# Three places for a split w_q tile, and its low parts summed by a DMA

## What is computed

```python
x = x + g1 * (merged @ w_out[layer])
hffn = rms_norm(x, norm_ffn[layer]) * (1.0 + sc2) + sh2
...
q = (hf @ w_q).reshape(t, PEER_HEADS, 2, PEER_QDIM // 2)     # w_q: 1024 x 2048
s = jnp.einsum('thsd,hskd->thsk', q, subkeys)
top_s, top_i = lax.top_k(s, PEER_TOPK)
...
act = gelu(einsum('thkd,td->thk', u_tab[experts], h)); out = einsum('thk,thkd->td', gate * act, v_tab[experts])
```

## Time and profile before

| | |
|---|---|
| Time, median of 3 runs | 2116.46 us (2115.54 to 2118.68) |
| The profiled execution | 2115.24 us, its span 2113.5 us |
| Granted TensorE clock, mean | 0.989 |
| TensorE busy | 2022.2 us, 96% (weight loads 1734.9 us, 82%) |
| VectorE busy | 1572.1 us, 74% |
| ScalarE busy | 974.8 us, 46% |
| GpSimd busy | 265.2 us, 13% |
| DMA | 392.17 MB, 186 GB/s in the mean |

### The profile page before, as it was taken

How to read it: one execution, slowest core, us unless ns; L and a number is a source line. 1 busy time by engine, 2 the same in 40 slices (tenths; PEclk the granted TensorE clock), 3 DMA queues, 4 the chain that set the end, 5 groups by cost and what they waited for, 6 DMA issues and landing times.

```text
span 2113.5 us, 33847 instructions
## 1 busy us (share of the span) xinstructions
PE 2022.2 (96%) x11108; PEld 1734.9 (82%) x11108; DVE 1572.1 (74%) x3451; ACT 974.8 (46%) x1619; POOL 265.2 (13%) x309
## 2 busy tenths in 40 slices
PE   4998998899999999999999989999999999999998
PEld 3797988788888888888778989898888888888776
DVE  8884888676888888888666358996767676768854
ACT  3223337655444444444532142585555555554443
POOL 2002438400000000000010033590000000000000
PEclk9999999999999999999999999999999999999999
DMA  9376311355778877555443362114555565554562
GB/s 370 143 265 253 119 54 50 106 190 186 271 283 291 307 279 272 205 182 212 168 158 110 120 239 81 66 63 163 188 189 188 207 210 202 185 185 176 178 241 68
DMA packets 115738, 392.17 MB, mean 186 GB/s; under 512 B 12752, under 2 KB 20816, under 8 KB 115152
## 3 DMA queue, kind: packets, MB, share of 16 engines
q1 hardware_dynamic: 115664, 391.21, 51.8%
HBM read 384.35 MB, written 6.82 MB: 185 GB/s over the span
## 4 chain that ended last, share of the span: by engine, by line
PE 67%; DVE 21%; issue 5%; ACT 3%; DVEq 1%; DMA 1%; POOL 1%; SPq 0%
PE ps L890 25%; PE ps L881 13%; PE ps L883 6%; PE ps L624 5%; DVE v_lo L1698 4%; PE ps L852 3%; PE ps L637 3%; DVE next_w_ada_ring L1743 3%; PE ps L766 2%; DVE u_lo L1693 2%; DVE onehot_gate L1677 2%; DVE gated L1706 1%; PE ps L797 1%; ACT gelu L1242 1%; PE ps L792 1%
## 5 line engine op out<-in xcount | busy, mean ns | idle before, releaser
L881 PE MATMUL ps<-h_hi_lo,u_hi 128*128 128x512 f32 x1728 | 630.2, 399 | 6.3 <-DVE u_lo L1693 5.8
L883 PE MATMUL ps<-h_hi_lo,u_lo 128*128 128x256 f32 x1512 | 425.1, 281 | 0.0
L881 PEld LDWEIGHTS ps<-h_hi_lo,u_hi 128*128 128x128 f32 x1728 | 325.9, 189 | 76.6 <-issue 6.5
L883 PEld LDWEIGHTS ps<-h_hi_lo,u_lo 128*128 128x128 f32 x1512 | 286.7, 190 | 8.2
L890 PE MATMUL ps<-v_hi,gated_hi 128*128 128x512 f32 x864 | 271.9, 396 | 5.6 <-DVE gated_lo L1712 4.5
L1693 DVE TENSOR_TENSOR u_lo<-weight_ring,u_hi 128x1024 fp32r<-128x1024 f32 x216 | 263.6, 1221 | 14.9 <-ACT u_hi L1231 11.1
L890 PE MATMUL ps<-v_lo,gated_hi 128*128 128x512 f32 x864 | 268.2, 392 | 0.0
L890 PE MATMUL ps<-v_hi,gated_lo 128*128 128x512 f32 x864 | 266.4, 389 | 0.0
L1698 DVE TENSOR_TENSOR v_lo<-weight_ring,v_hi 128x1024 fp32r<-128x1024 f32 x216 | 263.2, 1218 | 0.6 <-ACT v_hi L1236 0.6
L1236 ACT ACTIVATE v_hi<-weight_ring 128x1024 fp32r<-128x1024 f32 x216 | 227.4, 1053 | 55.6 <-PE ps L890 55.5
L1242 ACT ACTIVATE gelu<-gelu 128x256 f32<-128x256 f32 x216 | 90.3, 418 | 328.3 <-DVE gelu L1702 328.3
(11 more groups left out here) (315 smaller groups left out, 3094.9 us busy)
## 6 DMA issues: line engine op xcount, KB each, us to landing
weight_ring<-in_u_tab_dram SPq DMA_DIRECT2D x224, 512.0 KB, 4.5
weight_ring<-in_v_tab_dram SPq DMA_DIRECT2D x216, 512.0 KB, 3.5
next_w_ada_ring<-in_w_ada_dram SPq DMA_DIRECT2D x56, 512.0 KB, 4.5
weight_ring<-in_w_in_dram SPq DMA_DIRECT2D x46, 512.0 KB, 3.6
w_ada_ring<-in_w_ada_dram SPq DMA_DIRECT2D x40, 512.0 KB, 8.9
v_tail<-in_v_tab_dram SPq DMA_DIRECT2D x40, 512.0 KB, 4.5
weight_ring<-in_w_q_dram SPq DMA_DIRECT2D x32, 512.0 KB, 3.5
u_ahead<-in_u_tab_dram SPq DMA_DIRECT2D x22, 512.0 KB, 8.6
```

The lines of the kernel that those rows point to most:

```text
L881: last = mm(both, UH[:, b, k, :], HB[:, :, k, :], start=(k == 0), stop=(k == KT - 1))
L883: mm(PS[:, 4 + b, 0:T], UL[:, b, k, :], HH[:, k, :], start=False, stop=False)
```

## The change

`w_q_hi` and `w_q_lo` get three places each. ScalarE writes the high part and then, from the same tile with scale -1, the negated high part into `w_q_lo`. GpSimd no longer subtracts: for each tile it issues a DMA that reads the tile from DRAM again and adds it onto what stands in `w_q_lo`. TensorE waits for that DMA's semaphore, one for each place. The ring's place is free once ScalarE is done. ScalarE works three tiles ahead: tile 2 after the activations' high parts, tile n+3 after the eviction of query n, and tile 1 between squares 5 and 6 of the norm. Because `w_q_lo` now covers the place of the first late expert tile, `ahead_late(0)` is issued after 15 queries.

In all five norms the sum of squares has its operands exchanged: the squares are the weights (two halves of 128 tokens), one column of ones is moving, and the sums come out as one value per token, so that VectorE needs one small operation in place of two reductions.

```diff
@@ -198,8 +198,8 @@
         SCR = at("scratch_row", 43008, [P, D])
         ANGLE = [at("angles", 44032, [P, 4, T]), at("next_angles", 28672, [P, 4, T])]
         TURNS = [at("turns", 10240, [P, 4, T]), at("next_turns", 29696, [P, 4, T])]
-        WQH = at("w_q_hi", 38912, [P, 2, KT, P], F32R)
-        WQL = at("w_q_lo", 40960, [P, 2, KT, P], F32R)
+        WQH = at("w_q_hi", 38912, [P, 3, KT, P], F32R)
+        WQL = at("w_q_lo", 41984, [P, 3, KT, P], F32R)
         OHA = at("onehot_gate", 38912, [P, 4, 4, P])
         OHB = at("onehot_key", 40960, [P, 4, 4, P])
         GE = at("gelu", 51200, [P, 2, T])
@@ -312,7 +312,7 @@
         in_ssm = sem("in_ssm_tables")
         ident_ready = sem("ident_bf16_ready")
         wq_hi = sem("w_q_hi_done")
-        wq_split = sem("w_q_split")
+        wq_low = [sem(f"w_q_low_summed_{i}") for i in range(3)]
         f_done = sem("ssm_factors_done")
         act_step = sem("scalar_step")
         pool_step = sem("gpsimd_step")
@@ -372,6 +372,10 @@
             n = (NSTREAM + 1) // 4 - (1 if slot == 3 else 0)
             return slot, l * full - (l if slot == 3 else 0) + n + 1
 
+        def w_q_low(l, n):
+
+            return wq_low[n % 3], 16 * (l * len(range(n % 3, 16, 3)) + n // 3 + 1)
+
         LATE_STORES = [len(range(i, A_GATE, 4)) for i in range(4)]
 
         def ahead_loaded(l, a):
@@ -422,7 +426,7 @@
                         elif m < TILE_Q:
                             sp.wait_ge(wo_mm, l * KT + m - TILE_OUT + 1)
                         else:
-                            sp.wait_ge(wq_split, l * 16 + m - TILE_Q + 1)
+                            sp.wait_ge(wq_hi, l * 16 + m - TILE_Q + 1)
                     if n < TILE_OUT:
                         src = w_in[l, IN_ORDER[n]]
                     elif n < TILE_Q:
@@ -483,7 +487,6 @@
                         sp.wait_ge(cond_kept, 16)
                         for a in range(A_TOP):
                             sp.dma_start(RAWU[a][:, :, :], u_tab[l, NM + a].rearrange("p (k n) -> p k n", n=P)).then_inc(in_ahead[a // 2], 16)
-                        ahead_late(0)
 
                 for v in (0, 1):
                     for e in (0, 1):
@@ -491,11 +494,13 @@
                         last = NSTREAM - 1 - (NSTREAM - 1 - slot) % 4
                         if slot == 3:
                             break
-                        sp.wait_ge(wq_split, l * 16 + last - TILE_Q + 1)
+                        sp.wait_ge(wq_hi, l * 16 + last - TILE_Q + 1)
                         sp.dma_start(RING[:, slot, :], (v_tab if v else u_tab)[l, e]).then_inc(in_ring[slot], 16)
 
-                sp.wait_ge(wq_split, l * 16 + 13)
+                sp.wait_ge(wq_hi, l * 16 + 13)
                 ahead_late(1)
+                sp.wait_ge(q_mm, l * 16 + 15)
+                ahead_late(0)
                 sp.wait_ge(ahead_gelu, l * AHEAD + 8)
                 sp.dma_start(KEPT[l, :, 0:8, :], GEA[:, 0:8, :]).then_inc(kept_most, 16)
                 sp.wait_ge(ahead_gelu, l * AHEAD + A_TOP)
@@ -589,7 +594,9 @@
                 bank = 4 * (n % 2)
                 for k in ks:
                     pe.wait_ge(squared, n * KT + k + 1)
-                    last = mm(PS[:, bank, 0:T], ONES[:, :], SQ[:, k, :], start=(k == 0), stop=(k == KT - 1))
+                    for t in range(TT):
+                        last = mm(PS[:, bank + t, 0:1], SQ[:, k, t * P:(t + 1) * P], ONES[:, 0:1], start=(k == 0),
+                                  stop=(k == KT - 1))
                 if k == KT - 1:
                     last.then_inc(sumsq, 1)
 
@@ -793,14 +800,15 @@
                     last.then_inc(ahead_mm, 1)
                 def query(n, k):
 
-                    b, out = n % 2, PS[:, 4 + n % 2, 0:T]
+                    b, out = n % 3, PS[:, 4 + n % 2, 0:T]
                     mm(out, WQH[:, b, k, :], HH[:, k, :], start=(k == 0), stop=False)
                     mm(out, WQH[:, b, k, :], HL[:, k, :], start=False, stop=False)
                     return mm(out, WQL[:, b, k, :], HH[:, k, :], start=False, stop=(k == KT - 1))
 
                 for n in range(16):
                     if n == 0:
-                        pe.wait_ge(wq_split, l * 16 + 2)
+                        pe.wait_ge(*w_q_low(l, 0))
+                        pe.wait_ge(*w_q_low(l, 1))
                         for k in range(KT):
                             pe.wait_ge(h_split, l * KT + k + 1)
                             for b in range(2):
@@ -808,7 +816,7 @@
                                 if k == KT - 1:
                                     last.then_inc(q_mm, 1)
                     elif n >= 2:
-                        pe.wait_ge(wq_split, l * 16 + n + 1)
+                        pe.wait_ge(*w_q_low(l, n))
                         pe.wait_ge(q_ev, l * 16 + n - 1)
                         for k in range(KT):
                             last = query(n, k)
@@ -980,10 +988,10 @@
 
 
                 for n in range(16):
-                    slot, _ = ring_pos(l, TILE_Q + n)
                     pool.wait_ge(wq_hi, l * 16 + n + 1)
-                    gp.tensor_tensor(WQL[:, n % 2, :, :], RING[:, slot, :].rearrange("p (k n) -> p k n", n=P),
-                                     WQH[:, n % 2, :, :].bitcast(F32), ALU.subtract).then_inc(wq_split, 1)
+                    gp.dma_start(WQL[:, n % 3, :, :], w_q[l, n].rearrange("p (k n) -> p k n", n=P),
+                                 accum_op=ALU.add).then_inc(wq_low[n % 3], 16)
+
 
 
 
@@ -1038,7 +1046,9 @@
 
                 slot, value = ring_pos(l, TILE_Q + n)
                 act.wait_ge(in_ring[slot], value)
-                fn(WQH[:, n % 2, :, :], RING[:, slot, :].rearrange("p (k n) -> p k n", n=P), ACT.Copy).then_inc(wq_hi, 1)
+                raw = RING[:, slot, :].rearrange("p (k n) -> p k n", n=P)
+                fn(WQH[:, n % 3, :, :], raw, ACT.Copy)
+                fn(WQL[:, n % 3, :, :], raw, ACT.Copy, scale=-1.0).then_inc(wq_hi, 1)
 
             def norm(n):
 
@@ -1046,12 +1056,12 @@
                     if n == 0:
                         act.wait_ge(in_x, 16)
                     else:
+                        if n % 2 and k == 6:
+                            w_q_high(n // 2, 1)
                         act.wait_ge(x_ready, (n - 1) * KT + k + 1)
                     fn(SQ[:, k, :], X[:, k, :], ACT.Square).then_inc(squared, 1)
                 act.wait_ge(var_done, n + 1)
                 fn(RS[:, :], RS[:, :], ACT.Sqrt).then_inc(std_done, 1)
-                if n % 2:
-                    w_q_high(n // 2, 1)
 
             def shift(n, which):
                 for k in range(KT):
@@ -1163,6 +1173,7 @@
                 for k in range(KT):
                     act.wait_ge(normed, (2 * l + 1) * KT + k + 1)
                     fn(HH[:, k, :], HT[:, k, :], ACT.Identity, bias=MODS[l][:, SH2, k:k + 1]).then_inc(h_hi, 1)
+                w_q_high(l, 2)
                 def gelu_ahead(a):
                     act.wait_ge(ahead_mm, l * AHEAD + a + 1)
                     fn(GEA[:, a, :], PS[:, 2 + a % 2, 0:T], ACT.Gelu_apprx_tanh).then_inc(ahead_gelu, 1)
@@ -1171,8 +1182,8 @@
                     if n >= 2:
                         act.wait_ge(ks_mm, l * 16 + n - 1)
                     fn(QT[:, n % 2, :], PS[:, 4 + n % 2, 0:T], ACT.Copy).then_inc(q_ev, 1)
-                    if n + 2 < 16:
-                        w_q_high(l, n + 2)
+                    if n + 3 < 16:
+                        w_q_high(l, n + 3)
                     if n < 4:
                         for k in (2 * n, 2 * n + 1):
                             last = fn(H32[:, k, :], HT[:, k, :], ACT.Identity, bias=MODS[l][:, SH2, k:k + 1])
@@ -1301,13 +1312,9 @@
 
                 dve.wait_ge(sumsq, n + 1)
                 bank = 4 * (n % 2)
+                v.tensor_scalar(RS[:, :], PS[:, bank:bank + TT, 0], 1.0 / D, EPS, ALU.mult, ALU.add).then_inc(var_done, 1)
                 if n == 0:
                     dve.wait_ge(in_const, 16)
-                for t in range(TT):
-                    last = v.tensor_tensor_reduce(out=DIAG[:, t, :], in0=PS[:, bank, t * P:(t + 1) * P], in1=IDENT[:, :],
-                                                  scale=1.0 / D, scalar=EPS, op0=ALU.mult, op1=ALU.add,
-                                                  accum_out=RS[:, t:t + 1])
-                last.then_inc(var_done, 1)
                 dve.wait_ge(std_done, n + 1)
                 link(v.reciprocal(RS[:, :], RS[:, :]))
                 for t in range(TT):
```

## The result

The changed kernel takes 2133.01 us (median of five, 2129.64 to 2137.35), the kernel before 2116.46 beside it: 16.6 us between the medians. The ratio on record is 1.0089, 95% interval 1.0076 to 1.0103; it is not that of these two medians (1.0078) and stands for 18.8 us. The forecast was slower by 7.3 us: the sign is right, the size is less than half of what was measured.

The account below looks back on a forecast made before the run. TensorE, busy 96% of the span, was taken to bound the kernel. Layer 0's query stage +6.7, layer 1's +1.6 and three other norms -1.05 made +7.3 us on 2115.24, so 2122.5, as median 2123.7 us; range 2110 to 2136.

Parts of the forecast that it names:

- c: Query stage: time one adding transfer takes from the sixteen DMA engines, taken as 2.0 us, bounds 1.28 and 2.56.
- L: Query stage: time from ScalarE's signal to TensorE's through an adding transfer, taken as 5.0 us (3.5 to 6.5), 7 while queue full.
- what the steady stretch gives back: Query stage, later tiles: GpSimd's 0.37 us waits at tiles 8, 11 and 14 vanish, -1.1 us per layer.
- the price of the norms: Five norms: VectorE saves 0.35 us each, TensorE 0 with 0.3 either way; the three other norms sum to -1.05 us.
- tile 4 +6.3: Layer 0 query stage: lengthened queue lands tile 4 at 209.1, so query 4 starts at 216.1, not 209.77.
- the clock +1.5: Layer 0 query stage: TensorE's lower clock level after a pause, charged once more at +1.5 us; nothing in layer 1.
- Layer 1, tile 4: Layer 1 query stage: tile 4 lands at 1248.4, query 4 starts at 1255.4, not 1252.69, +2.7 us.
- Query 2: Layer 0 query stage: tile 2's low part is there at 202.7; query 3 ends 5 us before query 4 may start.
- ScalarE's second copy in layer 1: Norm before layer 1's queries: tile 0's extra 0.96 us copy is covered by 1.96 us; otherwise costs at most 0.96.
- Low transfers up to 8.1 us are hidden from tile 6 on: Query stage: 10.6 us of TensorE work between queries n and n+3, less 2.4 us of ScalarE copies, hides the transfer.
- always slow: Rival: with L beyond 8.1 us every round of three tiles waits; at L = 12, +48, 2165 us; chance 0.07.
- The prediction's last rival: Layer 0: tile 2's low part lands about 209, query 4 +7.3 instead of +6.3, forecast holds; no chance given.

Follow-up runs that it names:

- e4: The changed kernel with the old norm statistic and low transfers that copy w_q without adding; the same kernel with adding transfers is 1.06% (22.4 us) slower.
- g4: The changed kernel with ScalarE's two copies swapped, negated high part first, so the adding transfer is issued earlier; ratio 1.0060 to the kernel before.
- f2: The kernel of e1 with the statistic's one VectorE operation split into two one-column instructions; 0.13% slower than the kernel before.
- e2: The changed kernel with the old norm statistic put back (16 matmuls of 256 columns, two VectorE reductions); 2142.0 us.
- e1: The kernel before with only the new norm statistic (32 one-column matmuls, one VectorE operation); 2109.6 us.
- f3: The kernel before with two single-column memsets of an unused place on VectorE ahead of the first norm's statistic; layer 0's gates stage took 95.7 us.

## Why the prediction was right in sign and wrong in size

The mechanism was right: the adding transfers lengthen the queue ahead of tile 4, and the stage waits for tile 4. Three terms were mis-sized, c, L and what the steady stretch gives back; the price of the norms had the wrong sign. Forecast against the profiled executions: layer 0's query stage +6.7, measured +11.7; layer 1's +1.6, measured +14.2; the norms -1.05, measured +4; the gates stage nothing, measured -9.1. Within the stage, layer 0: tile 4 +6.3, measured +9.8; the clock +1.5, measured +1.5; the steady stretch -1.1, measured +0.35. Layer 1: +2.7, measured +12.1; 0, measured +1.8; -1.1, measured +0.35. In order of the prediction's steps:

- *c, the engine time of an adding transfer.* This is the step that failed first. I took 2.0 us between bounds of 1.28 and 2.56, "if the engines must also read the destination". Measured: 2.87 us, outside the bounds, against 1.52 for a copying one in e4. It is twice the 1.47 us that plain transfers cost by the same yardstick, so the doubling that I had as the dear end fits, and the choice of a value between the ends was what failed. Two and a half such transfers in the queue, less the load moved out of it, make 2.5 x 2.87 - 1.28 = 5.9 us; tile 4's load took 6.6 us longer in layer 0 and 7.7 in layer 1, so the way of counting was right and its price too low. That layer 0's landing came out near all the same (210.0, forecast 209.1) is luck: the load was issued 1.9 us earlier than I had it, since the 0.96 us of the second copy did not show. w_q tile 0 happened to land 1.2 us earlier than before (its copy begins at 174.61, before at 175.78). In layer 1 I had counted two transfers, since tile 1's would meet idle engines. It was issued at 1229.75 and landed 5.4 us later, and by then the u_ahead loads had begun.
- *L, from ScalarE's signal to TensorE's.* Taken as 5.0 (3.5 to 6.5). Measured: 7.19 and 6.83 us from issue to landing for tile 4 and a median of 7.9. In layer 0 the chain of the prediction then closes with the measured terms: landing 210.0, 2.3 us for ScalarE, 7.2 for the transfer, query 4 at 219.54. With 5.0 it would have been 217.3. The Trainium skill ("DMA: Bandwidth & Descriptors", Anatomy of one DMA) has a fit by which a plain transfer of this size takes 3.2 us, an estimate; e4's copying ones landed in 4.6 us at the median, the adding ones in 7.9, so it was right not to build on it.
- *Layer 1, tile 4.* Forecast 1255.4, measured 1269.6. Of these 14.2 us, 4.8 came from upstream, 7.2 from a later landing (2.2 of them because the load was issued later still, at 1238.98: the norm ran 1.3 us later, the issue of the eleven u_ahead loads took SyncE 6.83 us where it had taken 5.49, and 0.5 us of issuing ahead_late was gone; and 5.0 in the queue), and 2.2 from L and the copies.
- *Query 2.* I had it at 202.7, "matters less". It came at 204.12, after 5 us of pause, and it does not matter, as forecast: the chain of layer 0 does not pass it. TensorE was at the lower level after it (0.50 from 203 to 207), and again after tile 4's pause, in both layers. Only the second time costs: 1.5 us in layer 0, as charged, and 1.8 in layer 1, where I had charged nothing.
- *ScalarE's second copy in layer 1*, which 1.96 us were to cover, is on the chain (1224.77, then squares at 1225.72): about 1 us, the price given for the case that the cover fails. It failed because tile 0's load landed 1.65 us later against its surroundings than before (5.44 us after its issue, and not 3.8).
- *Low transfers up to 8.1 us are hidden from tile 6 on.* This holds: they landed in 5.3 to 9.1 us, those above 8.1 are tiles 6 to 8, and the pauses at tiles 7 and 8 are 0.46 and 0.20 us in layer 0, 0.22 and 0.35 in layer 1. The sign of being wrong that I had named, low transfers above 8 us from tile 6 on, did come up there, and the rival "always slow" had its condition met by so little that it had no price to speak of.
- *GpSimd's gaps at tiles 8, 11 and 14* are gone, but the -1.1 us a layer did not come: tiles 7 and 8 wait for their transfers instead, and the steady stretch takes 0.35 us more than before. In g4, whose transfers start 0.95 us earlier, it takes 0.9 us less than before in layer 0. h_low takes 0.48 us from the first, as forecast.
- *The norm.* "0, with 0.3 us either way" for TensorE was wrong: 5.64 us where it was 3.69, +2.1 us in norms 2 and 4, nothing to see in norm 0. The nearest row I had used, matmuls of 64 columns at 0.112 us, was taken at the full clock, and at the full clock a one-column matmul takes as long (0.12 us); in norms 2 and 4 they fell to 0.50, half of it. Yet the edit as a whole makes the kernel faster, for a reason that no working from its own operations could have found: VectorE has fewer instructions ahead of its loop. f2, which has the edit and the slow rhythm, is 0.13% slower than before, near 3 us.
- *The queue rule.* The prediction's last rival had a low transfer stand behind the whole queue. It did not: tile 2's, issued at 195.69, landed at 204.1, 5.9 us before the load that SyncE had issued at 188.71 behind eleven others. The Trainium skill ("DMA: Bandwidth & Descriptors", Queues, rings and completion order) has each engine take turns between its queues, and the trace agrees.

That the forecast range held the time owes much to luck: 26 us of loss and 4 from norms were offset by 9 from a stage outside the change. e2, with the slow gates stage, took 2142.0, outside the range of 2110 to 2136.

What stays open: whether an adding transfer takes twice the engine time because its destination is read as well, which fits the 2.87 us and which no run separates; why the two edits of the statistic, e1 and e2, differ by 4.4 and by 9 us; what delays the one instruction of VectorE; and why f3 went over to the slow rhythm.

## What to carry to other kernels

A DMA that adds is no free vector engine. Here it took 1.9 times the engine time of one that copies, landed 3 us later, and slowed the loads beside it. I take from it, beyond what these runs show, that it can pay only where its result is wanted late and the queues are idle; this stage has neither. When a change replaces a computation by a transfer, look at the first tiles, where the buffers' lead is not yet built up, before the steady stretch. And before a gain or loss of some 0.4% is put down to an edit, compare the stages that it did not touch: a loop shared by two engines may have two rhythms, and a few instructions more or less ahead of it can choose between them.

## What the runs showed of the hardware that was not expected

- An adding transfer of 512 KB: 2.87 us of all sixteen engines and 7.9 us to landing at the median; a copying one from the same queue 1.52 us and 4.6 us. With adding ones under way the full engines moved 239 to 312 GB/s, not 418.
- In norms 2 and 4 the granted clock fell to 0.50 under matmuls of one column, each with its own weight load, though TensorE was busy without a break (2121 to 2123), where 16 matmuls of 256 columns had kept it at 1.00 (2101 to 2103 before). In the norm before layer 1's queries, with other matmuls between its two halves, it stayed at 1.00.
- One instruction 0.27 us late in VectorE's loop set a stage shared with GpSimd to 96.7 us where it takes 87.5, to the end of the stage. The Trainium skill ("GPSIMD Engine Reference", Specifications) has GpSimd share its SBUF interfaces with VectorE, with contention where VectorE's instruction reads two inputs there or runs in a two-port mode; GpSimd's group of four at 4.19 us instead of 3.25, with VectorE's operations closer together, agrees with it and does not prove it.
